# Sorting small matmuls by tile size: chunk outputs of a DeltaNet/HGRN2 mixer and outputs of a state-space core

## The chip, the cores and the metric

The kernel is one program on one core of a Trainium2 chip. The metric is the device time of one execution in microseconds, lower is better. Five engines work side by side, each through its own list of instructions, and meet through semaphores: TensorE (PE), VectorE (DVE), ScalarE (ACT), GpSimd (POOL) and SyncE (SP), which here only issues DMAs. TensorE writes to eight PSUM banks of 128 partitions by 512 float32 values. All data are float32.

A few words are used throughout. A matmul multiplies a stationary operand (rows by columns, loaded by an LDWEIGHTS record) with a moving one (rows by N). The trace shows its shape as "128*64 128x128": a stationary operand of 128 rows and 64 columns, and a moving one of 128 rows and N = 128. A float32 matmul leaves two MATMUL records. Its **tile size** is the part of the array it takes: 128*128, 64*128, 128*64, 64*64 and so on. A **switch** is the passage from one tile size to another.

## The reference

One inference step of a two-layer hybrid decoder for 256 prompt tokens and 8 sequences of 8 sample tokens (T = 320 columns in all). Layer 0 mixes with four gated DeltaNet heads and four HGRN2 heads, layer 1 with a Mamba-2 state-space core (SSD) of 32 heads in 4 groups, and each is followed by a mixture of 16 experts. The two places that matter here are these lines of the recurrences over chunks of 64 tokens:

```python
# gated delta rule, one chunk: read of the state plus the products inside the chunk
o = (jnp.einsum('bthk,bhkv->bhtv', qc * jnp.exp(gam)[..., None], s)
     + jnp.einsum('bhts,bhsv->bhtv', qk, v_new))
# HGRN2, one chunk
o = (jnp.einsum('bthk,bhkv->bthv', qc * jnp.exp(cum), s)
     + jnp.einsum('btsh,bshv->bthv', att, vc))
# SSD, one chunk
y = jnp.einsum('btsgr,bsgrp->btgrp', cb[..., None] * seg * dtc[:, None], xc)
y = y + jnp.einsum('btgn,bgrpn->btgrp', cc, s) * jnp.exp(cum)[..., None]
```

## The kernel before, in words

Activations lie feature-major: 1024 features are eight tiles of 128 partitions by T columns. Every engine has one program written out by hand in the order in which it runs; there is no planner. PSUM is split in two rings of four banks. `bank_for_act` hands TensorE the next bank that ScalarE will empty, `bank_for_dve` the next one for VectorE. Each puts a wait in TensorE's list until the consumer has freed the use of that bank four banks before (`act_free`, `dve_free`), and the last matmul into a bank raises `act_full` or `dve_full`.

**Weights** stream from HBM in blocks of 1 MB into a ring of slots. SP issues a load as soon as TensorE has given its slot back (`weights_used`).

**Layer 0, the chunk loop** (end of `ab` in TensorE's program). Four chunks c = 0 to 3 are walked in order. For c > 0 TensorE first makes the product of the DeltaNet state (L996), updates of the sample states (L792, `sample_updates`) and one turn of conditioning (L712, `cond_turn`). Then for every c: `state_product` (L823, 4 matmuls), `chunk_outputs` for the DeltaNet heads, a wait for HGRN2 states, `chunk_outputs` for the HGRN2 heads, and `cond_product` (L698: 8 matmuls of 32 columns by N = 512, which use two slots of weights). VectorE turns the state product into the next state (L2067) and subtracts in `v_new` (L2056); ScalarE copies the outputs out (L1532). In `chunk_outputs` each of four heads has its 64 columns of the bank. For c > 0 a head has two matmuls that accumulate: the state read (L813, 128*128, N = 64) and the product inside the chunk (L814, 64*128, N = 64), head after head. For c = 0 there is no state and only L814 is there.

**Layer 1, the SSD core** (`ssd` in TensorE's program). It runs `front(0)`, and then for each group of heads gi = 0 to 3: `front(gi + 1)`, `back(gi)` and, from gi = 1, `norm_of_group(gi - 1)`. `front` begins with L1079 and `norm_of_group` is L1072 (four matmuls of 128*128, N = 320). `back(gi)` has, in this order, the reads of the sample states (L1118), the prompt's state product (L1125), eight products for the states of the eight sequences (L1130, a DVE bank each), a wait for the decay matrices (`att_ready`), and the outputs. VectorE's `back` mirrors this: L2154, then the decay matrices (L2156 to L2158), then for each of the eight sequences a multiply (L2162) and an add that frees the bank (L2164), and at last for each of the four output banks L2172, which frees it, and L2173.

The outputs of one group are four banks j of two heads each. A bank takes 9 matmuls: one of 128*128, N = 64 (L1135, the sample reads for both heads), two of 64*64, N = 64 (L1139, one per head in its half of the partitions), and six of 128*64, N = 128: L1141, L1143 and L1145, two each. L1141 and L1143 have the same stationary operand and the left and right half of the 256 prompt columns; L1145 accumulates onto L1143's columns. The banks are taken one at a time: TensorE waits for bank j, fills it, and goes on to j + 1.

The code around the change:

Of the kernel before, what the change touches and what calls it, by code (L numbers as in the profile page):

```python
# [25 lines left out]
P = 128  # L26
D = 1024
DK = D // P
PROMPT = 256
SEQS, SEQ_LEN = 8, 8  # L30
T = PROMPT + SEQS * SEQ_LEN
C = 64
# [9 lines left out]
HEADS = 4  # L42
# [21 lines left out]
BANK = 512  # L64
# [120 lines left out]
def trunk_program(nc, a, out):  # L185
    with ExitStack() as ctx:
# [74 lines left out]
        hk, hv, hq, hf, zs, hg = (lo(B) for _ in range(6))  # L261
# [39 lines left out]
        def half(o):  # L301
            return slice(o * C, (o + 1) * C)

        def tok(buf, i, o):

            if i < TILE_BLOCKS:
                at = i % HEADS * T + i // HEADS * P + o * C
            else:
                at = (2 * (i - TILE_BLOCKS) + o) * T + PROMPT
            return buf[:, at:at + C]  # L310

        def col(buf, i, w, parts=slice(0, P)):
            return buf[parts, i * w:(i + 1) * w]
# [323 lines left out]
        def _(pe):  # L637
            n = Count()

            def bank_for_act():  # L640
                i = n.n.get(id(act_full), 0)
                if i >= BANKS:
                    pe.wait_ge(act_free, n.at(act_full, 1 - BANKS))
                n.up(act_full)
                return psum[i % BANKS]
# [157 lines left out]
                        mm = pe.matmul(b[:, hp * C:(hp + 1) * C], col(v, i, P, half(o)), col(att, i, C, half(o)), start=False, stop=True)  # L803
                    mm.then_inc(act_full, 1)

            def chunk_outputs(c, state, q, v, att):

                tile, o = divmod(c, 2)
                b = bank_for_act()
                for hh in range(HEADS):  # L810
                    i = tile * HEADS + hh
                    if state is not None:
                        pe.matmul(b[:, hh * C:(hh + 1) * C], state[:, hh * P:(hh + 1) * P], tok(q, i, o), start=True, stop=False)  # L813
                    mm = pe.matmul(b[:, hh * C:(hh + 1) * C], col(v, i, P, half(o)), col(att, i, C, half(o)), start=(state is None), stop=True)  # L814
                mm.then_inc(act_full, 1)

            def state_product(c, kend, v):

# [7 lines left out]
            def ab():  # L826
# [162 lines left out]
                for c in range(PC):  # L989
# [12 lines left out]
                        cond_turn()  # L1002
                        pe.wait_ge(v_new_ready, c)
                    state_product(c, KEND, UTOK)
                    chunk_outputs(c, S[c % 2] if c else None, QT, UTOK, QKE)
                    if c:
                        pe.wait_ge(hgrn_states, c)
                    else:
                        pe.wait_ge(gla_ready, 1)
                    chunk_outputs(c, HS0[c - 1] if c else None, hq, VTOKH, ATT)  # L1010
                    cond_product()
                sample_updates(3, KM, UTOK)
                cond_turn()
# [24 lines left out]
            def ssd():  # L1038
# [70 lines left out]
                def back(gi):  # L1109
# [20 lines left out]
                        pe.matmul(bank_for_dve()[:, :], BM[q][rows_, a_ * P:(a_ + 1) * P], XEND[q][rows_, 2 * BANK:3 * BANK],  # L1130
                                  start=True, stop=True).then_inc(dve_full, 1)
                    pe.wait_ge(att_ready, gi + 1)
                    for j in range(4):
                        b = bank_for_dve()
                        pe.matmul(b[:, PROMPT:T], YS[:, j * P:(j + 1) * P], SK("strip_token"), start=True, stop=False)  # L1135
                        heads = [(slice(o * C, (o + 1) * C), 2 * j + o) for o in range(2)]
                        xh = lambda c, hh, parts=P: XDT[q][0:parts, c * BANK + hh * C:c * BANK + (hh + 1) * C]
                        for rows_, hh in heads:
                            pe.matmul(b[rows_, PROMPT:T], xh(2, hh, C), es[:, hh, :], start=False, stop=True)  # L1139
                        for rows_, hh in heads:  # L1140
                            pe.matmul(b[rows_, 0:P], xh(0, hh), e0[:, hh, 0:P], start=True, stop=True)  # L1141
                        for rows_, hh in heads:
                            pe.matmul(b[rows_, P:PROMPT], xh(0, hh), e0[:, hh, P:PROMPT], start=True, stop=False)  # L1143
                        for rows_, hh in heads:
                            mm = pe.matmul(b[rows_, P:PROMPT], xh(1, hh), e1_[:, hh, :], start=False, stop=True)  # L1145
                        mm.then_inc(dve_full, 1)

                front(0)
# [1417 lines left out]
```

## Time and profile before

| | us |
|---|---|
| median of three runs | 1596.0 (1578.27 to 1607.25) |
| profiled execution | 1592.63 |
| its span in the trace | 1590.7 |
| TensorE busy | 1402.4 (88%) |
| VectorE busy | 557.5 (35%) |
| ScalarE busy | 253.0 (16%) |
| mean granted TensorE clock, share of full | 0.899 |

Busy TensorE time counts an instruction from its start to its modelled end, and neighbours overlap; it says how long the engine had work, not how well the work filled it. Where two instructions follow each other, the distance of their starts is the price of the first. The granted clock is 1.00 or 0.50 at any moment (2.4 or 1.2 GHz); a value between is a stretch that holds some of each.

### The profile page before, as it was taken

The page shows a single profiled execution, that of the slowest core. Times are in us where ns is not written, and L with a number is a line of the kernel's source. Part 1 is how long each engine was busy: PE and PEld are TensorE (multiplying, and loading weights), DVE is VectorE, ACT ScalarE, POOL GpSimd, SP SyncE. Part 2 cuts the span into 40 slices and gives each one's busy share as a digit, 9 for nine tenths or more (in the row PEclk, how much of TensorE's full clock was granted, in tenths as well). Part 3 has the DMA queues.
Part 4 walks back from the last instruction along what each step waited for, and adds up shares of the span by engine and source line. Part 5 has one row for each costly group of instructions (what it writes and reads, how often), then busy time and mean ns, then how long its engine had stood idle before and what let it go on. Part 6 is the DMA issues. An engine that isn't in the chain of part 4 may idle for free.

```text
span 1590.7 us, 19016 instructions
## 1 busy us (share of the span) xinstructions
PE 1402.4 (88%) x7784; PEld 787.6 (50%) x7784; DVE 557.5 (35%) x1233; ACT 253.0 (16%) x468; POOL 31.0 (2%) x28
## 2 busy tenths in 40 slices
PE   6798999979699999996899998889698599999984
PEld 2466777646453344433566664444366344434432
DVE  0534654251501232223444003667701502322233
ACT  2233232020210001001232112122100110100001
POOL 0000000000000000000000002110000000000000
PEclk8899999679859999999899999667699669999997
DMA  9303143361759999895122723323340279989960
GB/s 391 151 1 123 57 157 115 113 265 57 303 226 393 383 380 381 340 402 227 53 106 106 273 106 106 102 91 126 146 206 0 96 286 397 380 340 381 380 277 34
DMA packets 53082, 336.29 MB, mean 211 GB/s; under 512 B 5136, under 2 KB 5648, under 8 KB 15488
## 3 DMA queue, kind: packets, MB, share of 16 engines
q1 hardware_dynamic: 51664, 323.65, 51.2%
q0 software_dynamic: 1328, 11.36, 1.9%
q8 instruction: 66, 1.08, 0.3%
q14 instruction: 24, 0.20, 0.0%
HBM read 319.02 MB, written 15.96 MB: 211 GB/s over the span
## 4 chain that ended last, share of the span: by engine, by line
PE 83%; DVE 9%; issue 3%; ACT 2%; DMA 1%; POOL 1%; SPq 0%; DVEq 0%; ACTq 0%; POOLq 0%
PE bank L681 26%; PE bank L1211 22%; PE bank L1194 8%; PE bank L1245 4%; PE bank L698 3%; PE bank L730 2%; PE bank L752 2%; PE bank L1130 2%; PE bank L712 1%; DMA pool<-w_ada_in 1%; PE bank L814 1%; DVE h L1759 1%; PE bank L1255 1%; DVE x L2284 1%; PE bank L1072 1%
## 5 line engine op out<-in xcount | busy, mean ns | idle before, releaser
L681 PE MATMUL bank<-h,pool 128*128 128x320 f32 x1280 | 362.3, 442 | 10.1 <-ACT pool L1442 3.3
L1211 PE MATMUL bank<-pool 128*32 128x512 f32 (+1 forms) x2304 | 342.9, 599 | 12.2 <-DVEq L1726 6.1
L681 PEld LDWEIGHTS bank<-h,pool 128*128 128x128 f32 x1280 | 244.9, 194 | 117.7 <-issue 16.9
L1211 PEld LDWEIGHTS bank<-pool 128*32 128x32 f32 (+1 forms) x2304 | 107.3, 119 | 230.4 <-issue 217.1
L1194 PE MATMUL bank<-pool 128*128 128x256 f32 (+1 forms) x384 | 131.1, 478 | 10.8 <-issue 10.8
L1194 PEld LDWEIGHTS bank<-pool 128*128 128x128 f32 (+1 forms) x384 | 73.5, 221 | 63.6 <-issue 58.2
L1245 PE MATMUL bank<-pool 128*128 128x320 f32 x256 | 76.1, 442 | 9.4 <-PE bank L1211 6.9
L681 PE MATMUL bank<-pool 128*128 128x320 f32 x256 | 72.5, 447 | 5.4 <-DVEq L1726 5.0
L2284 DVE SCALAR_TENSOR_TENSOR x<-bank,mod,x 128x256 f32<-128x256 f32 x64 | 30.7, 480 | 125.3 <-PE bank L1245 125.3
L2284 DVE SCALAR_TENSOR_TENSOR x<-bank,pool,x 128x256 f32<-128x256 f32 x64 | 30.7, 480 | 125.2 <-PE bank L1245 125.1
L698 PE MATMUL bank<-pool,cs 128*32 128x512 f32 x384 | 58.4, 730 | 16.6 <-DMA small<-small_in 11.1
L1245 PEld LDWEIGHTS bank<-pool 128*128 128x128 f32 x256 | 46.2, 190 | 50.8 <-issue 31.1
L681 PEld LDWEIGHTS bank<-pool 128*128 128x128 f32 x256 | 50.2, 197 | 27.6 <-DVEq L1726 5.5
L1800 DVE SCALAR_TENSOR_TENSOR pool<-pool,small 128x344 f32<-128x344 f32 x108 | 62.3, 577 | 3.8
L1651 ACT ACTIVATE pool<-bank 128x512 f32<-128x512 f32 x32 | 19.1, 597 | 272.0 <-PE bank L1194 272.0
L2301 DVE TENSOR_TENSOR pool<-bank,pool 128x512 f32<-128x512 f32 x16 | 11.1, 692 | 112.6 <-PE bank L1211 112.6
L1130 PE MATMUL bank<-pool 32*128 32x512 f32 x64 | 29.9, 883 | 20.7 <-DVE pool L2164 20.0
L1798 DVE TENSOR_SCALAR pool<-pool,small 128x344 f32<-128x344 f32 x36 | 14.4, 399 | 93.0 <-ACTq L1355 92.7
L730 PE MATMUL bank<-h,const 128*128 128x320 f32 x80 | 30.1, 542 | 18.2 <-ACT h L1362 18.2
L1675 ACT ACTIVATE pool<-bank 128x512 f32<-128x512 f32 x32 | 17.4, 595 | 160.5 <-PE bank L1211 160.5
L1748 DVE TENSOR_TENSOR pool<-bank,small 128x36 f32<-128x36 f32 x12 | 2.4, 196 | 97.8 <-PE bank L712 97.5
L698 PEld LDWEIGHTS bank<-pool,cs 128*32 128x32 f32 x384 | 11.9, 123 | 47.7 <-issue 29.8
(398 smaller groups left out, 1293.6 us busy)
## 6 DMA issues: line engine op xcount, KB each, us to landing
pool<-moe_w_gate_in SPq DMA_DIRECT2D x64, 1024.0 KB, 9.8
pool<-moe_w_up_in SPq DMA_DIRECT2D x64, 1024.0 KB, 10.8
pool<-moe_w_down_in SPq DMA_DIRECT2D x64, 1024.0 KB, 7.4
pool<-w_ada_in SPq DMA_DIRECT2D x48, 1024.0 KB, 9.3
pool<-ssd_w_in_in SPq DMA_DIRECT2D x20, 1024.0 KB, 6.5
pool<-ab_w_in_in SPq DMA_DIRECT2D x16, 1024.0 KB, 23.7
pool<-ssd_state_in SPq DMA_DIRECT2D x4, 2048.0 KB, 11.1
ssd_s_out<-pool SPq DMA_DIRECT2D x4, 2048.0 KB, 7.2
```

The source lines that it names most:

```text
L681: mm = pe.matmul(b[:, 0:T], ws[kk // 4][:, kk % 4, mt * P:(mt + 1) * P], rhs[:, kk * T:(kk + 1) * T], start=(kk == 0), stop=(kk == nk - 1))
L698: mm = pe.matmul(b[kk * STRIP:(kk + 1) * STRIP, :], cs[:, (k0 + kk) * STRIP:(k0 + kk + 1) * STRIP], w[:, kk, :], start=(k0 == 0), stop=(k0 ...
L730: mm = pe.matmul(b[:, 0:T], ones, h[:, kk * T:(kk + 1) * T], start=(kk == 0), stop=(kk == DK - 1))
L752: mm = pe.matmul(b[half(o), (i - first) * width:(i - first + 1) * width], lhs(i, o), rhs(i, o), start=True, stop=True)
L1130: pe.matmul(bank_for_dve()[:, :], BM[q][rows_, a_ * P:(a_ + 1) * P], XEND[q][rows_, 2 * BANK:3 * BANK], start=True, stop=True).then_inc(dv ...
L1194: mm = pe.matmul(b[:, q * PAIR:(q + 1) * PAIR], HTOK[0:k_, c * D + (k0 + q) * P:c * D + (k0 + q + 1) * P], OH[0:k_, c * PAIR:(c + 1) * PAI ...
L1211: mm = pe.matmul(b[at:at + w_, :], lhs(kk0 + kk)[:, at:at + w_], ws[e][:, o_:o_ + BANK], start=(first and kk == 0), stop=(last and kk == p ...
L1245: pe.matmul(b[:, 0:T], YE[p_ % 2][:, kk * P:(kk + 1) * P], PT, start=True, stop=True).then_inc(dve_full, 1)
L1651: act.activation(XT[j % 2][:, o_:o_ + BANK], b[:, :], ACT.Copy).then_inc(act_free, 1)
L1675: act.activation(YE[p_ % 2][:, i * BANK:(i + 1) * BANK], b[:, :], ACT.Copy).then_inc(act_free, 1)
L1800: ins = stt(cv, up[:, j:j + CVW], w[:, f * TAPS + j:f * TAPS + j + 1], cv, ALU.mult, ALU.add)
L2284: stt(xk, b[:, 0:PROMPT], modv[:, 40 + kk, 0:1], xk, ALU.mult, ALU.add)
```

## The change

`chunk_outputs` takes both mixers at once. It takes both banks first, issues the eight state reads of 128*128 (both mixers), and then the eight products of 64*128. The wait for the HGRN2 states now stands ahead of all of them. Only the first matmul into a bank carries the start flag; the other heads' first products write where the bank is still clear.

In the SSD outputs TensorE takes all four banks of a group ahead of the first matmul. The four products of 128*128 come first, then the eight of 64*64, then bank by bank those of 128*64. The two of 128 columns with one stationary operand (L1141, L1143) become one of N = 256, so a group has 28 matmuls where it had 36. Each bank still raises `dve_full` at its own last matmul. Nothing else changes.

```diff
--- before.py
+++ after.py
@@ -803,16 +803,18 @@
                         mm = pe.matmul(b[:, hp * C:(hp + 1) * C], col(v, i, P, half(o)), col(att, i, C, half(o)), start=False, stop=True)
                     mm.then_inc(act_full, 1)
 
-            def chunk_outputs(c, state, q, v, att):
+            def chunk_outputs(c, mixers):
 
                 tile, o = divmod(c, 2)
-                b = bank_for_act()
-                for hh in range(HEADS):
-                    i = tile * HEADS + hh
-                    if state is not None:
-                        pe.matmul(b[:, hh * C:(hh + 1) * C], state[:, hh * P:(hh + 1) * P], tok(q, i, o), start=True, stop=False)
-                    mm = pe.matmul(b[:, hh * C:(hh + 1) * C], col(v, i, P, half(o)), col(att, i, C, half(o)), start=(state is None), stop=True)
-                mm.then_inc(act_full, 1)
+                banks = [bank_for_act() for _ in mixers]
+                for b, (state, q, v, att) in zip(banks, mixers):
+                    for hh in range(HEADS if c else 0):
+                        pe.matmul(b[:, hh * C:(hh + 1) * C], state[:, hh * P:(hh + 1) * P], tok(q, tile * HEADS + hh, o), start=(hh == 0), stop=False)
+                for b, (state, q, v, att) in zip(banks, mixers):
+                    for hh in range(HEADS):
+                        i = tile * HEADS + hh
+                        mm = pe.matmul(b[:, hh * C:(hh + 1) * C], col(v, i, P, half(o)), col(att, i, C, half(o)), start=(c == 0 and hh == 0), stop=(hh == HEADS - 1))
+                    mm.then_inc(act_full, 1)
 
             def state_product(c, kend, v):
 
@@ -1002,12 +1004,11 @@
                         cond_turn()
                         pe.wait_ge(v_new_ready, c)
                     state_product(c, KEND, UTOK)
-                    chunk_outputs(c, S[c % 2] if c else None, QT, UTOK, QKE)
                     if c:
                         pe.wait_ge(hgrn_states, c)
                     else:
                         pe.wait_ge(gla_ready, 1)
-                    chunk_outputs(c, HS0[c - 1] if c else None, hq, VTOKH, ATT)
+                    chunk_outputs(c, [(S[c % 2], QT, UTOK, QKE), (HS0[c - 1], hq, VTOKH, ATT)])
                     cond_product()
                 sample_updates(3, KM, UTOK)
                 cond_turn()
@@ -1130,19 +1131,19 @@
                         pe.matmul(bank_for_dve()[:, :], BM[q][rows_, a_ * P:(a_ + 1) * P], XEND[q][rows_, 2 * BANK:3 * BANK],
                                   start=True, stop=True).then_inc(dve_full, 1)
                     pe.wait_ge(att_ready, gi + 1)
-                    for j in range(4):
-                        b = bank_for_dve()
+                    banks = [bank_for_dve() for _ in range(4)]
+                    heads = [(slice(o * C, (o + 1) * C), o) for o in range(2)]
+                    xh = lambda c, hh, parts=P: XDT[q][0:parts, c * BANK + hh * C:c * BANK + (hh + 1) * C]
+                    for j, b in enumerate(banks):
                         pe.matmul(b[:, PROMPT:T], YS[:, j * P:(j + 1) * P], SK("strip_token"), start=True, stop=False)
-                        heads = [(slice(o * C, (o + 1) * C), 2 * j + o) for o in range(2)]
-                        xh = lambda c, hh, parts=P: XDT[q][0:parts, c * BANK + hh * C:c * BANK + (hh + 1) * C]
-                        for rows_, hh in heads:
-                            pe.matmul(b[rows_, PROMPT:T], xh(2, hh, C), es[:, hh, :], start=False, stop=True)
-                        for rows_, hh in heads:
-                            pe.matmul(b[rows_, 0:P], xh(0, hh), e0[:, hh, 0:P], start=True, stop=True)
-                        for rows_, hh in heads:
-                            pe.matmul(b[rows_, P:PROMPT], xh(0, hh), e0[:, hh, P:PROMPT], start=True, stop=False)
-                        for rows_, hh in heads:
-                            mm = pe.matmul(b[rows_, P:PROMPT], xh(1, hh), e1_[:, hh, :], start=False, stop=True)
+                    for j, b in enumerate(banks):
+                        for rows_, o in heads:
+                            pe.matmul(b[rows_, PROMPT:T], xh(2, 2 * j + o, C), es[:, 2 * j + o, :], start=False, stop=False)
+                    for j, b in enumerate(banks):
+                        for rows_, o in heads:
+                            pe.matmul(b[rows_, 0:PROMPT], xh(0, 2 * j + o), e0[:, 2 * j + o, :], start=False, stop=False)
+                        for rows_, o in heads:
+                            mm = pe.matmul(b[rows_, P:PROMPT], xh(1, 2 * j + o), e1_[:, 2 * j + o, :], start=False, stop=True)
                         mm.then_inc(dve_full, 1)
 
                 front(0)
```

## Rows read from the trace of the kernel before

**Rows 1.** The page: TensorE's busy time, granted clock in 40 slices, chain by engine.

```profile
...
PE 1402.4 (88%) x7784; PEld 787.6 (50%) x7784; DVE 557.5 (35%) x1233; ACT 253.0 (16%) x468; POOL 31.0 (2%) x28
...
PEclk8899999679859999999899999667699669999997
...
PE 83%; DVE 9%; issue 3%; ACT 2%; DMA 1%; POOL 1%; SPq 0%; DVEq 0%; ACTq 0%; POOLq 0%
```

**Rows 2.** Busy time and clock by stretch, layer 0 (the first line names the columns).

```profile
...
core 0: us, PE busy (x) PEld busy (x) DVE busy (x) ACT busy (x) POOL busy (x), PEclk, DMA share, GB/s
266.07:267.90 1.83, 1.83 (x19) 1.76 (x17) 1.48 (x4) 0.38 (x1) 0.00 (x0) 1.00 0.10 34
267.90:270.16 2.26, 1.93 (x18) 0.45 (x17) 2.11 (x4) 0.66 (x2) 0.00 (x0) 1.00 0.25 40
274.31:283.15 8.84, 8.84 (x33) 7.17 (x33) 1.64 (x7) 0.38 (x1) 0.00 (x0) 0.59 0.15 62
290.99:299.54 8.55, 8.55 (x33) 6.93 (x32) 1.63 (x7) 0.38 (x1) 0.00 (x0) 0.61 0.16 67
307.67:315.96 8.29, 8.29 (x33) 6.71 (x32) 1.64 (x7) 0.38 (x1) 0.55 (x1) 0.64 0.16 63
283.15:286.83 3.68, 3.34 (x17) 0.62 (x17) 0.00 (x0) 0.65 (x2) 0.00 (x0) 0.61 0.23 33
299.54:303.52 3.98, 3.65 (x18) 0.63 (x17) 0.00 (x0) 0.65 (x2) 0.00 (x0) 0.55 0.25 56
315.96:319.94 3.98, 3.65 (x18) 0.63 (x17) 0.00 (x0) 0.65 (x2) 0.00 (x0) 0.50 0.26 56
```

**Rows 3.** Timeline of TensorE, chunk 1: start, us, engine, line, shapes, records.

```profile
...
274.31 0.44 PE L813 MATMUL bank<-pool 128*128 128x64 f32 x2
274.68 0.43 PE L814 MATMUL bank<-pool 64*128 64x64 f32 x2
```

**Rows 4.** Timeline of VectorE, chunk 1: the update of the DeltaNet state.

```profile
...
275.01 1.12 DVE L2067 SCALAR_TENSOR_TENSOR pool<-pool,bank 128x128 f32<-128x128 f32 x4
```

**Rows 5.** Waits of SP's queue, 255 to 480 us: for whom, total us, times, longest.

```profile
...
SPq L501 <- PE bank L698: 107.0, 8, 33.7
```

**Rows 6.** Timeline of TensorE and VectorE, SSD outputs of group 0, first bank.

```profile
...
1015.71 0.69 PE L1135 MATMUL bank<-pool 128*128 128x64 f32 x2
...
1016.33 0.48 PE L1139 MATMUL bank<-pool 64*64 64x64 f32 x4
...
1016.74 0.69 PE L1141 MATMUL bank<-pool 128*64 128x128 f32 x4
...
1017.22 0.64 PE L1143 MATMUL bank<-pool 128*64 128x128 f32 x4
...
1017.65 0.64 PE L1145 MATMUL bank<-pool 128*64 128x128 f32 x4
...
1018.22 0.69 PE L1135 MATMUL bank<-pool 128*128 128x64 f32 x2
1018.27 0.69 DVE L2164 TENSOR_TENSOR pool<-bank,pool 128x512 f32<-128x512 f32 x1
```

**Rows 7.** Busy time and clock by stretch, SSD outputs and what follows them.

```profile
...
1015.71:1025.74 10.03, 10.03 (x73) 7.76 (x73) 6.30 (x11) 0.00 (x0) 0.00 (x0) 0.50 0.54 207
...
1127.51:1137.53 10.02, 10.02 (x73) 7.76 (x72) 6.29 (x11) 0.00 (x0) 0.00 (x0) 0.50 0.55 210
1025.74:1030.24 4.50, 4.50 (x20) 3.32 (x19) 2.19 (x6) 0.49 (x1) 0.00 (x0) 0.51 0.56 137
1066.57:1071.21 4.64, 4.64 (x11) 3.08 (x10) 1.04 (x2) 0.00 (x0) 0.00 (x0) 0.51 0.21 51
1107.27:1110.36 3.09, 3.09 (x14) 1.94 (x16) 1.04 (x2) 0.00 (x0) 0.00 (x0) 0.77 0.28 40
1137.53:1140.85 3.32, 3.32 (x10) 1.99 (x8) 1.04 (x2) 0.00 (x0) 0.00 (x0) 0.72 0.01 4
```

**Rows 8.** Timeline of VectorE, group 1: its first operation of back.

```profile
...
1041.64 0.69 DVE L2154 TENSOR_TENSOR pool<-bank,pool 128x512 f32<-128x512 f32 x1 [6.68 <-PE bank L1118]
```

## Prediction

> **What bounds the kernel now.** I read the page first. TensorE is busy 88% of the span and holds 83% of the chain that ended last, and its granted clock is below full in several slices [rows 1]. So time is gained where TensorE's list gets shorter, or where its clock stays up, as long as nobody else ends a wait there. The next view is the busy time by stretch of the chunk loop of layer 0 [rows 2]: in the outputs of chunks 1, 2 and 3 TensorE is busy all the time (8.84 of 8.84, 8.55 of 8.55, 8.29 of 8.29 us), VectorE has 1.6 us of work and ScalarE 0.4. TensorE bounds this place alone. The third view is the timeline of the SSD outputs [rows 6] with its stretches [rows 7]: there too TensorE is busy without a gap, 10.03 us in group 0 and 10.02 in group 3 (the two between are alike), all of it at a granted clock of 0.50. What follows a group hangs on the end of its outputs: VectorE waits 6.68 us for TensorE ahead of the next group's first operation [rows 8], so an end that moves, moves everything.
>
> **Chunk outputs, the switches.** Chunk 0 has eight products of 64*128, N = 64, and no state reads. They take 1.83 us at full clock, 0.23 us each [rows 2]. In chunk 1, at the start, where the clock is still full, a state read of 128*128 and a product of 64*128 follow each other at 0.37 us [rows 3]. Same N, same 128 columns to load: the difference of 0.14 us is the switch. After the change a chunk has eight state reads in a row and eight products in a row. At 0.23 each that is 16 x 0.23 = 3.7 us, and with a switch in the middle some 3.8 us. I take the price of an unswitched 128*128 product from that of the 64*128 one, since both load 128 columns and move 64; bounds are 0.23 and 0.37.
>
> **Chunk outputs, the clock.** Now the clock falls inside each of the three stretches (0.59, 0.61, 0.64), and the following conditioning product pays too: 3.68, 3.98 and 3.98 us against 2.26 after chunk 0, whose outputs need no sorting and whose clock stayed at 1.00 [rows 2]. What TensorE did before it fell was a conditioning turn, four state products and a few alternating pairs. Sorted, the same stretch works more densely and is over in 3.8 us, so I take it that the clock stays at full level, as it did in chunk 0. The outputs then go from 8.84 + 8.55 + 8.29 = 25.7 us to 11.4: **14.3 us gained**. The conditioning products go from 11.6 to 3 x 2.26 = 6.8: **4.9 us gained**. Together 19.2 us. If the clock falls at the same moments as now (after 1.5 to 2.3 us of outputs), the products left over cost 0.46 instead of 0.23, the outputs come to 17.4 us, the conditioning stays as it is, and 8.3 us are gained. These are the two ends.
>
> **What the faster loop could meet.** A chunk shortens from 16.7 us to about 10.3. VectorE's update of the DeltaNet state, which the next chunk reads, starts at 275.01 and takes 1.12 us [rows 4]; the sorted outputs and the conditioning product would end at 274.31 + 3.8 + 2.26 = 280.4. It is 4 us early. If that cover were gone, up to 1 us per chunk would show. The wait for the HGRN2 states moves ahead of the DeltaNet outputs. VectorE makes those states ahead of the loop, and its queue has reached chunk 1's update by then, so it costs nothing; its cover is that order. The two banks for ScalarE are taken at once: ScalarE has 0.38 us of work in 8.8, so nothing waits. Weights: SP waits 107.0 us for these conditioning products [rows 5], and the DMA share is 0.15 during the outputs; the loads are ahead and are held back by TensorE, not the other way. The same wait makes the later loads start earlier when TensorE is earlier, so the gain is carried on.
>
> **SSD outputs, the switches.** At half clock one bank takes 18.22 - 15.71 = 2.51 us: 0.62 for L1135, 0.41 for L1139, 0.48 for L1141, 0.43 for L1143 and 0.57 for L1145 [rows 6]. L1143 stands between two of its own size: 0.43 is the unswitched price of a pair with N = 128, so L1141 and L1145 hold 0.05 + 0.14 = 0.19 us of switching. Twice the 0.23 of chunk 0 gives 0.46 for L1135 unswitched, and half of 0.43 gives 0.21 for the pair with N = 64. The three pairs make 1.29, the bank 1.96, which leaves 0.55 for three switches, again 0.18 to 0.19 each. A group has 12 switches now and 3 after: 9 x 0.19 = 1.7 us less, and the sorted block takes 10.03 - 1.7 = **8.3 us** at half clock, 5.1 us of that the 128*64 products at its end. Bounds: nothing saved, or 0.15 more per bank should the N = 64 pairs drop further.
>
> **The merged product.** L1141 and L1143 load the same operand twice. Their pair costs 0.43 at half clock for 128 columns moved. The four products of N = 320 that follow take 4.64 us at nearly the same clock [rows 7], which is 3.6 ns a column or 0.46 for 128. So two matmuls of 128*64 run side by side at the price of the moving columns alone; no load shows, and I cost the merge at nothing. The Trainium skill (TensorE: Matmul & The Clock Gate, Part 3, The mechanism) says that a weight load overlaps with products in flight only when their row group differs; by that rule the 32 loads saved would show, an estimate of 53 ns each by the page's load formula and so under 2 us in all. The trace speaks against it.
>
> **SSD outputs, the banks.** This is the part that costs. Now TensorE begins bank 0 at 1015.71, while VectorE is still freeing the banks of the eight sequence states: the last add (L2164) starts at 1018.27 and takes 0.69 [rows 6]. That bank is the one that output bank 3 needs. Now it is asked for only at about 1023.2; after the change it is asked for first. TensorE stands from 1015.71 to 1019.00, 3.29 us. Queued behind that wait is the whole block, and behind it `front` of the next group but one. VectorE, which has nothing else to do, idles until bank 0 is done and then works in the shade of the rest; its last bank comes at the end as now. Per group 3.29 - 1.7 = 1.6 us later, four groups: **6.3 us lost** at an unchanged clock.
>
> **SSD, the clock.** Half clock goes on past the outputs: 4.50 us at 0.51, 4.64 at 0.51, 3.09 at 0.77 and 3.32 at 0.72 in groups 0 to 3 [rows 7]. In the last three, four unbroken products of N = 320 brought the clock up within 1.4 to 4.6 us. The sorted block ends in 5.1 us of unbroken wide products, so the clock should come up inside it, near its end. Then what follows runs at full level. Half of the time at half clock comes back: 2.2 + 2.3 + 0.7 + 0.9 = 6.1 us, and perhaps 0.4 inside each block, 1.7. I take **8 us back**. Bounds: 0, and 10 if it rises early. SSD altogether: 6.3 - 8 = 1.7 us gained, between 4 gained and 13 lost (13.2 is the wait with nothing saved).
>
> **The sum.** 19.2 + 1.7 = 20.9 us. The profiled execution took 1592.63 us; that makes 1571.7. It stands 3.4 us below the median of the three runs shown, 1596.0, so the forecast for the median is **1575 us**.
>
> **Rivals.**
> First, the clock falls in the sorted chunk outputs as well. For it: 64*128 products use half of the array, and N = 64 moves few columns per load, sorted or not. Against it: chunk 0, which is made of nothing else, kept 1.00. Gain 8.3 + 1.7 = 10 us, 1586.
> Second, the chunk loop gains in full, but the wide end of the SSD block does not raise the clock. For it: the outputs hold wide products now and stay at 0.50 for 10 us in all four groups. Gain 19.2 - 6.3 = 12.9, 1583.
> Third, slower than before: the bank wait. The place is the first matmul of each SSD output block, the price up to 3.29 x 4 = 13.2 us if sorting saves nothing in the block and the clock stays down. It decides once the chunk loop gives less than that, that is with the clock falling there too: 13.2 - 8.3 = 4.9 lost, 1601. Both halves speak against rows above.
> Fourth, more than forecast: a loop shortened by a third also moves later falls of the clock, of which the slices show several [rows 1], and some vanish. 12 us on top would give 1563.
>
> **Chances.** Forecast 0.55, first rival 0.18, second 0.12, slower 0.05, more than forecast 0.10. Around each case lies the scatter of the runs: three runs of one kernel spread over 29 us, so the range around the cases is 1560 to 1592. 2% is 32 us, about what a measurement of this kernel can tell from no change: faster means below 1564, slower above 1628. The forecast lies well inside. Faster by over 2%: 0.12, from the fourth case and the scatter. Slower by over 2%: 0.02. Within: 0.86.
>
> **What would show each step.** The outputs of chunks 1 to 3 take 3.7 to 4.0 us each at a clock of 1.00, the conditioning product after them 2.26, and a chunk some 10.3. In the SSD TensorE idles about 3.3 us ahead of L1135's counterpart, released by VectorE's L2164, four times; the block then takes up to 8.3 us, its four 128*128 products about 0.46 each, its N = 256 pairs 0.86 at half clock. The clock reads above 0.55 in the block, and 1.00 in the first microseconds behind it. I am wrong if unswitched 128*128 products still stand 0.37 apart, if the clock falls in the chunk outputs, or if the wait for banks is much shorter than 3 us because VectorE turns out to be earlier.

## The result and the profile after

The changed kernel takes 1577.99 us (median of 20 runs, 1571.10 to 1582.90), the kernel before 1595.8 us in the same comparison (20 runs). The ratio is 0.9901, 95% interval 0.9876 to 0.9926: 15.8 us less, between 11.8 and 19.8 (the two medians lie 17.8 apart; where this text compares kernels it goes by the ratios). Forecast was 1575 us. The profiled execution took 1576.69 us with a span of 1574.7 us, 16.0 less than the span of before.

The page of the changed kernel, the lines that answer to those of before [rows 1]. TensorE is busy for 29.6 us less, and it holds a little less of the chain.

```profile
...
PE 1372.8 (87%) x7720; PEld 768.6 (49%) x7720; DVE 557.1 (35%) x1233; ACT 253.2 (16%) x468; POOL 31.0 (2%) x28
...
PEclk8899999979769999998899999778699669999998
...
PE 81%; DVE 10%; issue 4%; ACT 2%; DMA 1%; POOL 1%; SPq 0%; DVEq 0%; ACTq 0%; POOLq 0%
```

To see where the 16.0 us of span lie, both programs are cut at the same instructions: the first chunk output, the first sample update behind the chunk loop, VectorE's first operation of group 0's `back`, and the first output-projection matmul of layer 1. First the kernel before, by stretch (the first line names the columns), then the changed kernel.

```profile
...
core 0: us, PE busy (x) PEld busy (x) DVE busy (x) ACT busy (x) POOL busy (x), PEclk, DMA share, GB/s
0.00:266.07 266.07, 230.08 (x1912) 158.72 (x1913) 116.26 (x221) 76.45 (x140) 4.12 (x11) 0.95 0.36 140
266.07:319.94 53.87, 52.53 (x299) 36.05 (x297) 17.22 (x49) 5.12 (x12) 0.55 (x1) 0.72 0.36 128
319.94:1000.81 680.87, 613.56 (x3099) 335.94 (x3100) 204.41 (x505) 109.03 (x224) 12.97 (x10) 0.93 0.60 240
1000.81:1150.24 149.43, 121.78 (x557) 65.90 (x557) 109.55 (x152) 22.76 (x31) 12.43 (x6) 0.71 0.33 120
1150.24:1590.70 440.46, 384.46 (x1922) 190.99 (x1922) 110.03 (x306) 39.58 (x62) 0.96 (x1) 0.91 0.62 252
```

```profile
...
0.00:271.84 271.84, 235.83 (x1912) 161.73 (x1913) 116.26 (x221) 76.49 (x140) 4.11 (x11) 0.92 0.35 137
271.84:306.72 34.88, 33.55 (x298) 25.85 (x297) 17.23 (x49) 5.13 (x12) 0.55 (x1) 1.00 0.52 192
306.72:987.38 680.66, 613.31 (x3099) 335.48 (x3100) 204.43 (x505) 109.06 (x224) 12.96 (x10) 0.93 0.60 240
987.38:1135.29 147.91, 106.77 (x492) 54.68 (x492) 109.16 (x152) 22.77 (x31) 12.43 (x6) 0.75 0.34 121
1135.29:1574.70 439.41, 383.36 (x1922) 190.84 (x1922) 110.02 (x306) 39.70 (x62) 0.96 (x1) 0.91 0.62 253
```

The chunk loop goes from 53.87 to 34.88 us (19.0 less), the SSD core from 149.43 to 147.91 (1.5 less). The middle and the tail give 0.2 and 1.1. Ahead of the loop, where both programs issue the same instructions, this execution is 5.8 us later, at a mean clock of 0.92 against 0.95. So the two changed places gave 20.5 us, and 4.5 us of that are gone elsewhere. At the end of the loop the changed kernel is 13.2 us ahead (306.72 against 319.94), not 19.

The chunk outputs and conditioning products of the changed kernel by stretch; they answer to [rows 2].

```profile
...
271.84:273.67 1.83, 1.83 (x19) 1.76 (x17) 1.48 (x4) 0.38 (x1) 0.00 (x0) 1.00 0.00 0
280.08:283.93 3.85, 3.85 (x33) 3.71 (x32) 1.64 (x7) 0.38 (x1) 0.00 (x0) 1.00 0.32 130
290.35:294.20 3.85, 3.85 (x34) 3.72 (x33) 1.63 (x7) 0.38 (x1) 0.00 (x0) 1.00 0.35 145
300.61:304.46 3.85, 3.85 (x33) 3.72 (x32) 1.64 (x7) 0.38 (x1) 0.55 (x1) 1.00 0.47 193
283.93:286.19 2.26, 1.93 (x17) 0.44 (x17) 0.00 (x0) 0.65 (x2) 0.00 (x0) 1.00 0.17 22
304.46:306.72 2.26, 1.93 (x17) 0.45 (x17) 0.00 (x0) 0.65 (x2) 0.00 (x0) 1.00 0.36 56
```

Each of the three outputs takes 3.85 us where it took 8.84, 8.55 and 8.29, and the clock reads 1.00 in all of them and behind them. The conditioning product takes 2.26 us.

Most of this is the clock and not the switches. In the kernel before a pair of alternating matmuls took 0.73 us while the clock was still full (274.31 to 275.04 in its chunk 1, where [rows 3] begin), so the eight pairs of a chunk would take 5.8 us at full clock, and the sorted ones take 3.85. That is 2.0 us a chunk, 6 in all. The other 8 us of the outputs and the 4.9 of the conditioning products, 13 of the loop's 19, are there because the clock stayed at 1.00.

The SSD outputs of group 0 in the timeline of TensorE (start, duration, line, shapes, records, idle time and releaser); they answer to [rows 6].

```profile
...
1005.68 1.94 PE L1138 MATMUL bank<-pool 128*128 128x64 f32 x8 [3.32 <-DVE pool L2165]
1007.55 1.12 PE L1141 MATMUL bank<-pool 64*64 64x64 f32 x16
1008.60 1.12 PE L1144 MATMUL bank<-pool 128*64 128x256 f32 x4
1009.51 0.64 PE L1146 MATMUL bank<-pool 128*64 128x128 f32 x4
...
1013.67 0.70 PE L1080 MATMUL bank<-pool 128*128 128x256 f32 x2
```

TensorE stands for 3.32 us until VectorE has freed the last bank of the sequence states. It does so in all four groups. Then the block runs. By stretch, the four blocks and what follows each, against [rows 7]:

```profile
...
1005.68:1013.67 7.99, 7.99 (x57) 6.06 (x57) 2.96 (x6) 0.00 (x0) 0.00 (x0) 0.52 0.69 262
1045.91:1054.15 8.24, 8.23 (x56) 6.15 (x56) 3.12 (x6) 0.00 (x0) 0.00 (x0) 0.50 0.68 257
1086.06:1093.12 7.06, 7.06 (x57) 5.55 (x57) 2.27 (x5) 0.00 (x0) 0.00 (x0) 0.59 0.78 297
1116.08:1123.50 7.42, 7.42 (x57) 5.72 (x57) 2.62 (x5) 0.00 (x0) 0.00 (x0) 0.56 0.74 283
1013.67:1018.17 4.50, 4.50 (x40) 3.34 (x39) 3.98 (x9) 0.49 (x1) 0.00 (x0) 1.00 0.79 188
1054.15:1056.47 2.32, 2.32 (x11) 1.69 (x9) 1.04 (x2) 0.00 (x0) 0.00 (x0) 0.97 0.79 222
1093.12:1095.50 2.38, 2.38 (x14) 1.47 (x13) 1.71 (x4) 0.00 (x0) 0.00 (x0) 1.00 0.03 8
```

The blocks take 7.99, 8.24, 7.06 and 7.42 us where they took 10.0. The clock comes up inside the block in groups 0, 2 and 3 (0.52, 0.59, 0.56) and right behind it in group 1, and what follows reads 1.00, 0.97 and 1.00 where it read 0.51, 0.51 and 0.77. The first of these stretches is as long as before, 4.50 us, but holds 40 matmul records where it held 20. From the end of the block to the first L1097 (L1096 in the kernel before), the same instructions, it is 2.86 us against 4.81. The four products of N = 320 behind group 1 take 2.32 us instead of 4.64.

### The profile page after: what moved, and what is told of

Its sections match the earlier page's. It is cut to its first block, busy times and chain, and to the rows that moved or that the text cites. A ratio compares the mean times of both kernels' runs of the same rounds, so it can differ in the third digit from the quotient of the medians.

```text
span 1574.7 us, 18892 instructions
## 1 busy us (share of the span) xinstructions
PE 1372.8 (87%) x7720; PEld 768.6 (49%) x7720; DVE 557.1 (35%) x1233; ACT 253.2 (16%) x468; POOL 31.0 (2%) x28
## 4 chain that ended last, share of the span: by engine, by line
PE 81%; DVE 10%; issue 4%; ACT 2%; DMA 1%; POOL 1%; SPq 0%; DVEq 0%; ACTq 0%; POOLq 0%
PE bank L681 27%; PE bank L1212 22%; PE bank L1195 8%; PE bank L1246 4%; PE bank L698 3%; PE bank L730 2%; PE bank L752 2%; PE bank L712 1%; DVE pool L2163 1%; DMA pool<-w_ada_in 1%; DVE h L1760 1%; PE bank L1256 1%; DVE x L2285 1%; PE bank L1144 1%; DVE pool L2157 1%
## 5 line engine op out<-in xcount | busy, mean ns | idle before, releaser
L681 PE MATMUL bank<-h,pool 128*128 128x320 f32 x1280 | 367.2, 447 | 10.1 <-ACT pool L1443 3.3
L698 PE MATMUL bank<-pool,cs 128*32 128x512 f32 x384 | 53.6, 675 | 16.6 <-DMA small<-small_in 11.2
L1131 PE MATMUL bank<-pool 32*128 32x512 f32 x64 | 29.7, 870 | 20.9 <-DVE pool L2165 20.2
L730 PE MATMUL bank<-h,const 128*128 128x320 f32 x80 | 31.0, 557 | 18.5 <-ACT h L1363 12.3
L1363 ACT ACTIVATE h<-x 128x2560 f32<-128x2560 f32 x5 | 11.7, 2336 | 144.4 <-DVEq L1727 143.9
```

Of the source, the lines that this page charges most:

```text
L681: mm = pe.matmul(b[:, 0:T], ws[kk // 4][:, kk % 4, mt * P:(mt + 1) * P], rhs[:, kk * T:(kk + 1) * T], start=(kk == 0), stop=(kk == nk - 1))
L698: mm = pe.matmul(b[kk * STRIP:(kk + 1) * STRIP, :], cs[:, (k0 + kk) * STRIP:(k0 + kk + 1) * STRIP], w[:, kk, :], start=(k0 == 0), stop=(k0 ...
L730: mm = pe.matmul(b[:, 0:T], ones, h[:, kk * T:(kk + 1) * T], start=(kk == 0), stop=(kk == DK - 1))
```

## Experiments

Two theories stand against each other. **Mine** is the sum of the prediction: switches and clock in the chunk loop, and in the SSD core a wait for banks that is paid back by fewer switches and an earlier clock. **The rival** is that the gain comes from where the clock happens to fall in the rest of the program. A second question is whether the clock in the sorted loop stays up by density or by shortness.

### One part alone

The first kernel has only the edit of `chunk_outputs`, the second only that of the SSD outputs (the halves of the diff shown ahead of the prediction).

> Only chunk_outputs is sorted; the SSD outputs are those of the kernel before. My theory (two parts that add up, nearly all of the gain in the chunk loop): the loop takes 34.9 us as in the changed kernel (53.9 before), the SSD core 149.4 us from VectorE's first operation of group 0's back to the first output-projection matmul, and the time is 19 us under before, some 1577. Rival (the gain comes from where the clock happens to fall elsewhere): the loop saves 19 us but the total keeps less than half of it. Rival (the SSD part carries more than 1.5 us of the gain): 1580 or more.

Measured: 1581.51 us, before 1596.46, ratio 0.9913 (0.9887 to 0.9938). The SSD core takes 149.2 us as before. The time is above 1580, the line of the second rival, but the missing microseconds are not in the SSD part; they are in the loop, as shown below.

> Only the SSD outputs are sorted with four banks taken first; the chunk outputs are those of before. My theory: the wait for banks (3.3 us per group, 13.2) and what it is paid back with (1.9 us less in each block, earlier rise of the clock) cancel to 1.5 us: total 1594, ratio 0.999, not told from before. Rival (the wait costs more than it brings): 1600 or above. Rival (sorting alone is worth it there): below 1590.

Measured: 1593.64 us, ratio 0.9987 (0.9972 to 1.0003); SSD core 148.0 us, loop 53.9. So the SSD part alone can't be told from no change, and the loop carries nearly all of the gain. But the loop of the first kernel did not take 34.9 us. Its loop and the outputs of its chunk 1, and the loop in a second profile of the same kernel:

```profile
...
265.90:307.07 41.17, 39.83 (x298) 29.09 (x297) 17.23 (x49) 5.13 (x12) 0.55 (x1) 0.83 0.45 163
274.13:280.08 5.95, 5.95 (x34) 5.71 (x33) 1.64 (x7) 0.38 (x1) 0.00 (x0) 0.62 0.24 98
```

```profile
...
267.41:311.80 44.39, 43.03 (x298) 31.33 (x297) 17.24 (x49) 5.12 (x12) 0.55 (x1) 0.77 0.42 152
```

41.17 and 44.39 us. The clock fell within the sorted outputs (0.62 in chunk 1), and that takes 6 to 10 us of the 19 away. The first rival of the prediction happens, in some executions, though at a smaller price than the 11 us it named (the loop still gains 12.7 and 9.5 us of the 19). The expectation for the second profile was:

> A further look at the kernel with only the chunk outputs sorted: the loop takes 34.9 or about 41 us. If the latter belonged to this kernel, 41 again.

Two further profiles of the changed kernel itself:

> The changed kernel once more, unchanged. Five profiles with the sorted chunk loop took 34.88 us in four cases and 41.17 in one (the clock fell inside it). Theory (the sorted loop stands at the margin, and where the clock's changes fall within it differs between executions): 34.9 or about 41 us, the total 1572 to 1583. Rival (the 41 us belong to the kernel with only the chunks sorted): always 34.9.

> A further look at the changed kernel, for the loop's time only: 34.9 or about 41 us, as above. Ahead of the loop: chunk 0's outputs start at about 265.9 or at about 271.9 us, whichever kernel it is.

Measured: 1578.54 us (ratio 0.9900, 0.9862 to 0.9938) and 1579.88 us, the loop 34.88 and 34.92 us, the first chunk output at 272.35 and 272.14 us. All profiles side by side, with the mean granted clock from 165 to 190 us, in code that every kernel shares, some 80 us ahead of the loop:

| kernel | clock, 165 to 190 us | chunk 0's outputs start | loop |
|---|---|---|---|
| before | 1.00 | 266.07 | 53.87 |
| SSD outputs sorted alone | 1.00 | 265.66 | 53.9 |
| before, banks first (below) | 0.93 | 271.96 | 52.60 |
| changed, three profiles | 0.93 | 271.84, 272.35, 272.14 | 34.88, 34.88, 34.92 |
| changed, banks late (below) | 0.93 | 271.80 | 34.9 |
| changed, no merge (below) | 0.93 | 272.22 | 34.9 |
| changed, pairs of banks (below) | 0.93 | 266.52 | 34.88 |
| chunk outputs sorted alone, two profiles | 1.00 | 265.90, 267.41 | 41.17, 44.39 |
| changed, outputs issued twice (below) | 1.00 | 267.7 | 66.0 |
| changed, sorted within one mixer (below) | 1.00 | 265.59 | 45.85 |
| pairs, conditioning first (below) | 1.00 | 267.68 | 34.4 |

With the sorted outputs of the changed kernel, issued once, the loop took 34.9 us in six profiles and 41.2 and 44.4 in two. The six are those in which the clock had dropped between 165 and 190 us, and the two are those in which it had not. The kernel with the outputs issued twice fits too: its clock fell in chunk 1, before the first instruction that the changed kernel does not have, and it had not dropped before. So the fall does not belong to the kernel with sorted chunks alone. It goes with where the clock's earlier changes lie in the execution. That is a pattern over nine profiles and not an experiment, since no run sets those changes, and how often each case occurs in a kernel is not known. The old loop lost its clock in all nine chunks of its three profiles, also in the one that had the drop before it (52.60 us), so the drop alone does not give a loop at full clock; the sorting is needed as well.

The later start, 272 in place of 266 us, is also found in one kernel whose chunk loop is the old one (banks first), so it does not need the new loop. All three profiles of the changed kernel have both the late start and the loop at full clock. At the end of the loop the kernels with sorted outputs, issued once, are 8.1 to 18.5 us ahead of the profile of the kernel before (311.80 to 301.40 us against 319.94).

### Short or dense

For chunks 1 to 3 the sixteen matmuls are issued, and then once more:

```diff
...
         pe.matmul(b[:, hh * C:(hh + 1) * C], state[:, hh * P:(hh + 1) * P], tok(q, tile * HEADS + hh, o), start=(hh == 0), stop=False)
 for b, (state, q, v, att) in zip(banks, mixers):
+    for hh in range(HEADS if c else 0):
+        i = tile * HEADS + hh
+        pe.matmul(b[:, hh * C:(hh + 1) * C], col(v, i, P, half(o)), col(att, i, C, half(o)), start=False, stop=(hh == HEADS - 1))
+for b, (state, q, v, att) in zip(banks, mixers):
+    for hh in range(HEADS if c else 0):
+        pe.matmul(b[:, hh * C:(hh + 1) * C], state[:, hh * P:(hh + 1) * P], tok(q, tile * HEADS + hh, o), start=(hh == 0), stop=False)
+for b, (state, q, v, att) in zip(banks, mixers):
     for hh in range(HEADS):
...
```

> The changed kernel, with the sixteen matmuls of the chunk outputs of chunks 1 to 3 issued twice in a row (the second time starts the banks anew, so the result is the same). It asks whether the clock stays up because the sorted stretch is short or because it is dense enough. If dense enough: 7.7 us per chunk at a clock of 1.00, 11.6 us slower than the changed kernel, 1590. If only short: the clock falls inside the second half, the stretch takes over 9 us and the following conditioning product 3.3 to 4.0 us in place of 2.26; 15 us or more slower.

Measured: 1603.68 us against 1600.03, ratio 1.0010 (0.9975 to 1.0045), so some 17 us above the changed kernel by the two ratios, between 10 and 24 by their intervals, which does not tell 11.6 from 15 or more. Nine of the ten runs took 1600.5 to 1605.1 us and one 1581.56; that one was not profiled. In the profile, of a run of 1605.00 us, the loop takes 66.0 us, 31 more than in the changed kernel. The doubled outputs of chunks 2 and 3 by stretch:

```profile
...
297.89:309.51 11.62, 11.62 (x65) 11.20 (x64) 1.64 (x7) 0.38 (x1) 0.00 (x0) 0.64 0.04 15
318.24:329.75 11.51, 11.51 (x65) 11.09 (x64) 1.64 (x7) 0.38 (x1) 0.55 (x1) 0.64 0.08 31
```

11.62 and 11.51 us in place of twice 3.85, at a mean clock of 0.64, and half clock through the conditioning product behind it (3.98 us). Where the fall lies, the timeline shows: the state reads (L812) and products (L816) of the first sixteen, then the state reads of the second sixteen (L819), in chunks 1 and 2.

```profile
...
275.95 2.60 PE L812 MATMUL bank<-pool 128*128 128x64 f32 x16
278.48 3.67 PE L816 MATMUL bank<-pool 64*128 64x64 f32 x16
282.08 3.67 PE L819 MATMUL bank<-pool 128*128 128x64 f32 x16
...
297.89 2.00 PE L812 MATMUL bank<-pool 128*128 128x64 f32 x16
299.81 2.56 PE L816 MATMUL bank<-pool 64*128 64x64 f32 x16
302.31 3.67 PE L819 MATMUL bank<-pool 128*128 128x64 f32 x16
```

The first sixteen take 6.13 and 4.42 us, and 4.31 in chunk 3, where the changed kernel takes 3.85. So the clock had fallen before the second sixteen began, in all three chunks, and neither case of the expectation holds: not full clock throughout, and not a fall inside the second half. By an estimate from these starts and the 1.93 us of eight matmuls at full clock, it fell some 1.3 us into the outputs of chunk 1 and 3.3 to 3.4 us into those of chunks 2 and 3. Once down it stayed down through the rest of the doubled stretch. So sorted products of N = 64 do not keep the clock up, and my reason "denser" is not enough. That the stretch of the changed kernel stays at full clock because it is short is not shown either: here the clock fell within that same length.

### Sorted within one mixer

```diff
-chunk_outputs(c, [(S[c % 2], QT, UTOK, QKE), (HS0[c - 1], hq, VTOKH, ATT)])
+for mixer in ((S[c % 2], QT, UTOK, QKE), (HS0[c - 1], hq, VTOKH, ATT)):
+    chunk_outputs(c, [mixer])
```

> The changed kernel, but the chunk outputs are sorted within one mixer only: four state reads, four products, then the same for the other mixer. Two more switches per chunk, same matmuls. Theory of the switches: the outputs of a chunk take 3.85 + 2 x 0.14 = 4.1 us and the clock stays at 1.00; total within 1 us of the changed kernel plus 0.8. Rival (the clock hangs on the margin of this stretch): the clock falls in at least one of the three chunks and the loop loses 3 us or more.

Measured: 1587.86 us, ratio 0.9930 (0.9896 to 0.9964). The price of the switches holds: at full clock four matmuls and a switch take 1.04 us here, sixteen and two switches 3.85 in the changed kernel. Solved for both, that gives 0.22 us a matmul and 0.15 a switch. But the clock fell in all three chunks, the outputs took 6.51, 4.92 and 4.88 us, and the loop 45.85. Against the changed kernel that is 11.0 us, not 0.8: the rival of this expectation was right. (By the ratios the total is 4.6 us above the changed kernel, and the intervals overlap.) How much of it the two switches cause can't be told from one profile: the clock had not dropped between 165 and 190 us here, and in the three profiles of the table where that was so and the outputs were fully sorted, in the order of the changed kernel, the clock fell too.

### The wait for banks

The kernel before, with the order of its matmuls unchanged:

```diff
-for j in range(4):
-    b = bank_for_dve()
+banks = [bank_for_dve() for _ in range(4)]
+for j, b in enumerate(banks):
```

> The kernel before, with one change: the four banks of an SSD group are taken ahead of its first matmul; order of the matmuls as before. It isolates the wait. Theory: TensorE idles 3.3 us ahead of the block in each of the four groups, the block still takes 10.0 us at half clock, so 13 us slower than before, some 1609. Rival (the time comes back, since VectorE is free of other work when the last bank is done and what follows was not bound by TensorE): under 5 us slower.

Measured: 1608.28 us against 1600.03, ratio 1.0052 (1.0025 to 1.0080). The wait is there in full, as the waits of TensorE in the SSD core show (for whom, total us, times, longest):

```profile
...
PE bank L1135 <- DVE pool L2164: 13.3, 4, 3.3
```

The SSD core takes 162.80 us, 13.4 over before, as expected. The total moved by 8.3 only, 4.0 to 12.8 by its interval, just under the 13 expected; where the other 5 us went is not shown.

Now the same matmuls as in the changed kernel with the wait made smaller, first by taking each bank ahead of its own first matmul:

```diff
-banks = [bank_for_dve() for _ in range(4)]
+banks = []
...
-for j, b in enumerate(banks):
+for j in range(4):
+    b = bank_for_dve()
+    banks.append(b)
     pe.matmul(b[:, PROMPT:T], YS[:, j * P:(j + 1) * P], SK("strip_token"), start=True, stop=False)
```

> The changed kernel, but each of the four SSD banks is taken just ahead of its own first matmul; order and number of matmuls are unchanged. Theory: bank 3 comes free at the same moment, but three of the four 128*128 products are done by then, so the block ends 3 x 0.46 = 1.4 us earlier per group: 5.5 us under the changed kernel, some 1572.5; TensorE's idle time of 3.3 us shows as three shorter waits between the L1135-like products, 1.9 to 2.4 us in sum. Rival (the wait is covered by something else): same as the changed kernel.

Measured: 1574.14 us, ratio 0.9875 (0.9849 to 0.9900); SSD core 140.95 us, 7.0 under the changed kernel. Two waits are left in group 0, 1.27 us in sum where 1.9 to 2.4 were expected:

```profile
...
1003.73 0.69 PE L1140 MATMUL bank<-pool 128*128 128x64 f32 x2 [0.64 <-DVE pool L2167]
1005.05 0.69 PE L1140 MATMUL bank<-pool 128*128 128x64 f32 x2 [0.63 <-DVE pool L2167]
```

Then by sorting over two banks at a time:

```diff
-banks = [bank_for_dve() for _ in range(4)]
+for j0 in (0, 2):
+    banks = []
+    for j in (j0, j0 + 1):
+        b = bank_for_dve()
+        banks.append((j, b))
+        pe.matmul(b[:, PROMPT:T], YS[:, j * P:(j + 1) * P], SK("strip_token"), start=True, stop=False)
...
```

> The changed kernel, but the SSD outputs are sorted over two open banks at a time: banks 0 and 1, then 2 and 3, each bank taken just ahead of its first matmul. Six switches per group in place of three, and bank 3 is asked for some 4 us later. Theory (the wait for four banks costs 3.3 us a group): no wait of TensorE over 0.3 us ahead of the block, the block takes 8.13 + 3 x 0.19 = 8.7 us at half clock, ends 2.7 us earlier in each group, less 1 us where the clock rises later: 7 to 11 us under the changed kernel, some 1569. Rival (VectorE or the clock sets the end of the group anyway): within 3 us of 1578.

Measured: 1569.00 us, ratio 0.9846 (0.9817 to 0.9875); SSD core 136.41 us, 11.5 under the changed kernel. Its timeline in group 0:

```profile
...
996.41 1.34 PE L1141 MATMUL bank<-pool 128*128 128x64 f32 x4
...
1001.06 0.71 PE L1141 MATMUL bank<-pool 128*128 128x64 f32 x4
...
1003.53 0.70 PE L1080 MATMUL bank<-pool 128*128 128x256 f32 x2
```

No wait stands ahead of either pair, and the block ends 7.1 us after its start: three more switches, but the second pair, from 1001.06 on, takes 2.47 us where the first took 4.65, so the clock came up at its start, earlier than in the changed kernel, where the expectation had it come up later. By the ratios it is 8.8 us under the changed kernel, within the 7 to 11 expected. The kernel with banks taken late is 4.1 under the changed kernel; its interval overlaps those of both, so its totals alone tell it from neither, and its place between them rests on the SSD core.

### The merged product

```diff
-for rows_, o in heads:
-    pe.matmul(b[rows_, 0:PROMPT], xh(0, 2 * j + o), e0[:, 2 * j + o, :], start=False, stop=False)
+for at in (0, P):
+    for rows_, o in heads:
+        pe.matmul(b[rows_, at:at + P], xh(0, 2 * j + o), e0[:, 2 * j + o, at:at + P], start=False, stop=False)
```

> The changed kernel, but the merged SSD product of N = 256 is again two of N = 128 in the order left half for both heads, right half for both heads. Theory (loads are hidden behind the other half's matmul): each bank still takes 1.28 us at half clock, no difference, 1578. Rival (each load shows, 53 ns for each of the 32 more): 1.7 us slower in all, and a bank takes 1.39 us.

Measured: 1575.94 us, ratio 0.9845 (0.9801 to 0.9889), and the interval overlaps the changed kernel's, though this total is 8.9 us lower by the ratios, with nothing in the core to account for it. SSD core 147.93 us against 147.91. Its timeline, the four products of N = 128 (x8) and the next:

```profile
...
1009.92 0.64 PE L1147 MATMUL bank<-pool 128*64 128x128 f32 x4
1010.35 1.07 PE L1145 MATMUL bank<-pool 128*64 128x128 f32 x8
1011.20 0.64 PE L1147 MATMUL bank<-pool 128*64 128x128 f32 x4
```

A bank takes 1.28 us with and without the merge: the loads of the 32 further matmuls cost nothing.

### Conditioning product ahead of the outputs

```diff
 state_product(c, KEND, UTOK)
+cond_product()
...
 chunk_outputs(c, [(S[c % 2], QT, UTOK, QKE), (HS0[c - 1], hq, VTOKH, ATT)])
-cond_product()
...
+conditioning(COND_LATE[c:c + 1])
 outputs(OI, c)
 outputs(OIH, c)
-conditioning(COND_LATE[c:c + 1])
```

> The kernel with SSD outputs sorted over pairs of banks, and in the chunk loop the conditioning product (N = 512, four column tiles side by side) moved from behind the chunk outputs to between state product and chunk outputs; ScalarE empties in the same order. If the fall of the clock hangs on the row of sparse work from the conditioning turn to the outputs, the dense product in its middle breaks that row, and the loop takes 34.9 us in every execution: 1569 or up to 2 us below by the median, with less scatter. Rival (the outputs alone are sparse enough, wherever they stand): the clock falls as often or oftener, the loop 37 us or more. No new wait is expected: ScalarE copies the conditioning product out during the outputs, 4 us ahead of the turn.

Measured: 1565.34 us (six runs, 1563.12 to 1569.26), ratio 0.9818 (0.9780 to 0.9856). The interval overlaps that of the pairs alone (0.9817 to 0.9875), so a gain of the reordering is not shown, but its six runs spread over 6 us where those of the pairs spread over 18.5 (1560.27 to 1578.80); with six runs each that is a hint of less scatter and no more. The timeline of chunk 1:

```profile
...
276.02 1.93 PE L698 MATMUL bank<-pool,cs 128*32 128x512 f32 x16
278.27 1.97 PE L812 MATMUL bank<-pool 128*128 128x64 f32 x16 [0.33 <-PE bank L698]
280.17 2.00 PE L816 MATMUL bank<-pool 64*128 64x64 f32 x16
282.10 1.09 PE L998 MATMUL bank<-pool 128*64 128x128 f32 x8
```

The outputs stand between the conditioning product and the state product of the next chunk, and the clock is at 1.00 through the whole loop of this profile. From the first conditioning product to the sample updates behind the loop it is 34.4 us for the same work. In this profile the clock had not dropped between 165 and 190 us, and it is the only one of the five such profiles with sorted outputs in which the loop kept 1.00. That speaks for the order with the dense product in the middle, but one profile does not show it. This kernel beats the kernel before and the changed kernel, whose interval (0.9876 to 0.9926) lies above its own.

## Why the prediction was right, step by step

- **TensorE alone bounds the chunk loop**: right. No new wait appeared there; the loop is 19.0 us shorter, 19.2 were summed.
- **Switch 0.14 us, unswitched product 0.23**: right. 3.85 us per chunk for 3.8.
- **The clock stays at full level**: this came true in all three profiles of the changed kernel, but not for the reason given, and so in part by luck. "Denser" does not hold it: the same products, sorted alone or issued twice, lost the clock in 8 of the 9 chunks of three other profiles. In the prediction's comparison, chunk 0 kept 1.00, but it kept it in every profile, with the old loop too, so it said nothing about the chunks behind it. The chance of 0.18 for the first rival stands against three profiles in nine, and as a case that holds or does not hold for a whole kernel it was put wrongly.
- **Wait for banks 3.29 us a group**: 3.32 measured, four times, and 13.4 us for it alone.
- **Block 8.3 us at half clock**: 8.24 in group 1, which was at 0.50 throughout.
- **Clock comes up near the end of the block, 8 us back**: the core gained 1.5 us net of 13.3 us of waiting, so block and clock gave 14.8; forecast 14.9. By stretch, the blocks are 9.4 us shorter (8.5 forecast, 1.7 of that for an earlier clock) and what follows them 5.9 (6.1 forecast). One sign named for it was missed: the clock was to read above 0.55 in the block, and it read 0.52 and 0.50 in groups 0 and 1.
- **Merge costs nothing**: right, the SSD cores with and without it differ by 0.02 us. The Trainium skill (TensorE: Matmul & The Clock Gate, Part 3, The mechanism) says that a weight load overlaps with products in flight only when their row group differs. Taken by itself, that would have made the kernel without the merge slower, and the 0.02 us speak against it. The same section also lets a load ahead when it goes to the background weight buffer, which the prediction left out; whether that is what happened here no run shows.
- **Nothing else moves**: the sum has no term for the rest of the program (only the fourth rival did, and only as a gain), and this is what was off. The sum was 20.9 us; the two places gave 20.5 in the profile, and the measured gain is 15.8. In the profile 5.8 us are lost ahead of the loop in code that both kernels share, by the clock. All three profiles of the changed kernel have this later start, and the one profile of the kernel before does not, though a kernel with the old loop has it too. The drop in clock between 165 and 190 us that is part of this loss is also what goes with a loop at full clock, so the 19 us and the 5.8 us are perhaps not two separate things. Why it comes, and how often in each kernel, stays open.

The slower rival did not come about. The experiment with the banks alone shows the price it named in the SSD core: 13.4 us there, had sorting returned nothing, of which 8.3 (4.0 to 12.8) reached the total.

## What to carry to other kernels

Count switches of tile size in a row of small matmuls: at full clock one cost 0.14 us beside 0.22 us for the matmul itself. Sort over as many open banks as are free at that moment: two banks at a time, taken late, beat four taken at once by 11.5 us in the SSD core and 8.8 us in all. Look at a sparse stretch together with its neighbours: if the clock falls in it, what follows is paid at half clock as well (3.98 us in place of 2.26 for the conditioning product). And do not take one profile for the behaviour of the kernel: the same sorted instructions kept the clock in some executions and lost it in others.

## What was not expected of the hardware

TensorE can be busy without a gap and still lose its clock: sorted products of N = 64 held 1.00 in every chunk in six profiles, and in only one chunk of nine in three others. Which of the two it was went with whether the clock had dropped some 80 us earlier, in code that all these kernels share. And the executions of the changed kernel differ by 12 us with the same instructions (1571 to 1583). The profiles of the kernels with this loop point to the clock: ahead of the loop the same instructions took 266.1 us at a mean clock of 0.95 and 271.8 at 0.92, and the sorted loop 34.9, 41.2 or 44.4 us at 1.00, 0.83 and 0.77.
